# Four places for the high parts of weight slots, splits one slot further ahead, and an earlier expert output split

## What is computed

```python
def swiglu(t, w_gate, w_up, w_down):
    return (jax.nn.silu(t @ w_gate) * (t @ w_up)) @ w_down

def even_layer(...):
    u = rmsnorm(h, norm_mix);  proj = u @ w_in            # 9 slots of weights
    ...                                                   # mixing
    h = h + jnp.concatenate([y_a, y_b], axis=-1) @ w_out  # 4 slots
    return h + swiglu(rmsnorm(h, norm_ffn), ffn_wg, ffn_wu, ffn_wd)   # 33 slots

def odd_layer(...):
    u = rmsnorm(h, norm_mix);  proj = u @ w_in            # 12 slots
    ...
    h = h + jnp.concatenate([y_c, y_d], axis=-1) @ w_out  # 4 slots
    t = rmsnorm(h, norm_ffn).reshape(b * s, d)
    return h + moe_swiglu(t, router, moe_wg, moe_wu, moe_wd).reshape(b, s, d)

def moe_swiglu(t, router, w_gate, w_up, w_down):
    ...
    for e in range(N_EXPERTS):
        out = out + combine[:, e:e + 1].astype(t.dtype) * swiglu(t, w_gate[e], w_up[e], w_down[e])
    return out
```

## Time and profile before

| what | value |
|---|---|
| median of three runs | 2070.26 us |
| the profiled execution, its own time | 2068.16 us |
| its span in the trace | 2066.4 us |
| PE busy | 1895.6 us (92%) |
| DVE busy | 1449.9 us (70%) |
| ACT busy | 1134.7 us (55%) |
| chain that ended last | PE 82%, DVE 8%, ACT 4%, issue 3%, DMA 2% |
| read from memory | 464.58 MB, 225 GB/s over the span |
| mean granted TensorE clock | 0.959 of full speed |

### The profile page before, as it was taken

One profiled execution on the slowest core, in us unless ns is written; L12 is line 12 of the kernel. 1 busy time (PEld: TensorE's weight loads), 2 busy tenths in 40 slices (PEclk: granted clock), 3 DMA queues, 4 the chain that ended last, 5 costly groups with the idle time before them and its releaser, 6 DMA issues.

```text
span 2066.4 us, 27904 instructions
## 1 busy us (share of the span) xinstructions
PE 1895.6 (92%) x11188; PEld 1651.4 (80%) x11190; DVE 1449.9 (70%) x1458; ACT 1134.7 (55%) x1180; POOL 36.5 (2%) x84
## 2 busy tenths in 40 slices
PE   5969979999978699999999999999999997898997
PEld 4948869998867578788887888888888885888887
DVE  3777543445455478888888888888888886495484
ACT  4531223333344366776767676776766675554552
POOL 0010000000002000000000000000000000010010
PEclk9999989999999799999999999999999998899999
DMA  7200033454320378988889898888988895333331
GB/s 286 103 0 1 1 123 143 184 184 163 123 102 1 143 303 342 360 347 347 353 338 361 342 360 345 338 361 329 373 339 352 353 359 235 106 121 142 123 123 41
DMA packets 63775, 467.43 MB, mean 226 GB/s; under 512 B 7200, under 2 KB 7328, under 8 KB 7328
## 3 DMA queue, kind: packets, MB, share of 16 engines
q1 hardware_dynamic: 63648, 465.66, 57.9%
HBM read 464.58 MB, written 1.05 MB: 225 GB/s over the span
## 4 chain that ended last, share of the span: by engine, by line
PE 82%; DVE 8%; ACT 4%; issue 3%; DMA 2%; POOL 0%; SPq 0%; DVEq 0%; ACTq 0%
PE bank L511 80%; PE bank L521 2%; DMA weight_ring<-w_dram 2%; DVE split_ring L1693 1%; DVE squares L1679 1%; ACT split_ring L1214 1%; ACT moe_pair_high L1214 1%; ACT arena L1214 1%; DVE ycat L1677 1%; ACT L1214 1%; DVE expert_out_low L2190 0%; DVE moe_pair_low L2165 0%; DVE arena L1731 0%; DVE arena L1732 0%; ACT squares L1214 0%
## 5 line engine op out<-in xcount | busy, mean ns | idle before, releaser
L2165 DVE TENSOR_TENSOR moe_pair_low<-weight_ring,moe_pair_high 128x2048 fp32r<-128x2048 f32 x225 | 507.2, 2285 | 22.3 <-ACT moe_pair_high L1214 21.7
L1214 ACT ACTIVATE moe_pair_high<-weight_ring 128x2048 fp32r<-128x2048 f32 x225 | 426.6, 1916 | 37.5 <-DMA weight_ring<-w_dram 35.9
L511 PE MATMUL bank<-operand_high,split_ring 128*128 128x256 f32 x2000 | 399.9, 290 | 27.4 <-DVE operand_low L1700 22.1
L1214 ACT ACTIVATE arena<-bank 128x256 f32<-128x256 f32 (+5 forms) x250 | 114.3, 464 | 471.8 <-PE bank L511 442.6
L511 PE MATMUL bank<-moe_pair_high,operand_high 128*128 128x512 f32 x896 | 353.9, 395 | 9.1 <-DVE operand_low L2172 7.5
L511 PEld LDWEIGHTS bank<-operand_high,split_ring 128*128 128x128 f32 x2000 | 330.9, 197 | 31.7 <-issue 25.3
L511 PE MATMUL bank<-moe_pair_high,operand_low 128*128 128x512 f32 x896 | 352.6, 394 | 0.0
L511 PE MATMUL bank<-moe_pair_low,operand_high 128*128 128x512 f32 x896 | 350.1, 391 | 0.0
L1693 DVE TENSOR_TENSOR split_ring<-weight_ring,split_ring 128x2048 fp32r<-128x2048 f32 x78 | 178.4, 2290 | 211.5 <-ACT split_ring L1214 211.3
L511 PE MATMUL bank<-operand_low,split_ring 128*128 128x256 f32 x896 | 258.4, 288 | 0.0
L1214 ACT ACTIVATE split_ring<-weight_ring 128x2048 fp32r<-128x2048 f32 x78 | 148.9, 1912 | 159.2 <-PE bank L511 158.3
(11 more groups left out here) (283 smaller groups left out, 2661.8 us busy)
## 6 DMA issues: line engine op xcount, KB each, us to landing
weight_ring<-w_dram SPq DMA_DIRECT2D x381, 1024.0 KB, 6.9
arena<-w_dram SPq DMA_DIRECT2D x55, 1024.0 KB, 4.8
constants<-const_dram SPq DMA_DIRECT2D x1, 3124.0 KB, 17.8
parameters<-param_dram SPq DMA_DIRECT2D x1, 2896.5 KB, 24.2
hT<-x_dram SPq DMA_DIRECT2D x1, 1024.0 KB, 4.8
out_dram<-squares SPq DMA_DIRECT2D x1, 1024.0 KB, 3.9
constants<-const_dram SPq DMA_DIRECT2D x1, 128.0 KB, 4.6
parameters<-param_dram SPq DMA_DIRECT2D x1, 54.5 KB, 4.5
```

What stands on the lines that cost most here:

```text
L511: return pe.matmul(out, lhsT, rhs, start=start, stop=stop, skip_group_check=True)
L1214: return act.activation(out, in_, f, **kw)
L2165: tt(low_, raw_, high_.bitcast(F32), ALU.subtract).then_inc(moe_split, 1)
```

## The change

The high parts of all slots from 9 on get four places: the two of `late_high` and the two of `whi`. Slot n's high part so waits for slot n - 4 instead of n - 2. In the first output projection, the FFN and the second input projection, ACT and DVE take each slot's split one slot earlier. The extra split at the end of the first output projection is DVE's part of slot 15, behind `h_ready`; that at the FFN's end is slot 48's, behind slot 47's. In the second output projection one split fewer is left. In the experts' loop DVE's low parts of the output move ahead of the gate slot's low part. Loads, PE's program and the arithmetic are as before.

```diff
-            if not late and N_IN0 <= n < N_IN0 + 2:
-                return late_high[n - N_IN0]
+            if not late and n >= N_IN0:
+                return (late_high[0], late_high[1], whi[1], whi[0])[(n - N_IN0) % 4]
             return high_of[late][n % len(high_of[late])]
...
-                before = n - len(high_of[late])
+                before = n - (2 if n < N_IN0 and not late else 4)
                 if before >= 0 and (late or not N_IN0 <= n < N_IN0 + N_OUT):
                     act.wait_ge(*consumed[late, before])
...
-            for n in range(N_IN0 + 3, N_IN0 + N_OUT + 2):
+            for n in range(N_IN0 + 3, N_IN0 + N_OUT + 3):
                 hi(n)
             norm(1, 1)
             operand_hi(uT_, 1)
 
             w0 = N_IN0 + N_OUT
             for i in range(1, FFN_STEPS):
+                hi(w0 + 3 * i)
                 act.wait_ge(S["ffn_gu"], i)
-                hi(w0 + 3 * i - 1)
                 h = (i - 1) % 2
                 a_(sigb[h], banks[h][:, :], ACT.Silu).then_inc(S["ffn_sig"], 1)
-                hi(w0 + 3 * i)
                 hi(w0 + 3 * i + 1)
+                hi(w0 + 3 * i + 2)
             act.wait_ge(S["ffn_gu"], FFN_STEPS)
             a_(sigb[0], banks[0][:, :], ACT.Silu).then_inc(S["ffn_sig"], 1)
             w1 = w0 + N_FFN
-            hi(w1 - 1)
             hi(w1)
             hi(w1 + 1)
+            hi(w1 + 2)
...
-                    hi(w1 + 2 + 2 * i + n)
+                    hi(w1 + 3 + 2 * i + n)
...
             operand_hi(yc_)
-            hi(N_EARLY - 2)
             hi(N_EARLY - 1)
...
             st.say(dve.memset(tiny[:, 135:136], 0.0), "h_ready")
+            lo(N_IN0 + N_OUT + 2)
...
             for i in range(1, FFN_STEPS):
-                lo(w0 + 3 * i - 1)
+                lo(w0 + 3 * i)
                 ffn_step((i - 1) % 2, i)
-                lo(w0 + 3 * i)
                 lo(w0 + 3 * i + 1)
+                lo(w0 + 3 * i + 2)
             ffn_step(0, FFN_STEPS)
             w1 = w0 + N_FFN
-            lo(w1 - 1)
             lo(w1)
             dve.wait_ge(S["ffn_down"], FFN_STEPS + 1)
...
             lo(w1 + 1)
+            lo(w1 + 2)
...
-            for n in range(w1 + 2, w1 + N_IN1 + 2):
+            for n in range(w1 + 3, w1 + N_IN1 + 3):
                 lo(n)
...
-            residual(w1 + N_IN1 + 2)
+            residual(w1 + N_IN1 + 3)
...
                         moe_lo("down", q - 1)
-                    if q + 2 < QN:
-                        moe_lo("gate", q + 2)
                     if e and j == 1:
                         expert_out(e - 1)
                     if q + 2 < QN:
+                        moe_lo("gate", q + 2)
                         moe_lo("up", q + 2)
```

## The result

The changed kernel took 2048.44 us (median of 4 runs, 2047.08 to 2049.83) against 2068.84 us for the kernel before (4 runs, the three from above and one of 2067.41, 2062.81 to 2072.01): ratio 0.9905, 95% interval 0.988 to 0.9929. The prediction was 2050.5 us, in a range of 2043 to 2060. The profiled execution of after took 2047.08 us with a span of 2045.3, so 21.1 us less than the profiled one of before.

What follows compares the result with a forecast made beforehand. PE was taken as the bound, busy 1895.6 of 2066.4 us, so only its 171 idle us could be won. 4.8 + 6.1 − 2.3 + 0 + 9.0 = 17.6 us off 2068.16 gave 2050.5 us, range 2043 to 2060.

Steps and rivals of the forecast that it cites:

- (a): End of first output projection: slot 14 split earlier, less PE idle before the norm; gain 4.8 us, between 4.2 and 6.5.
- the commoner: Norm sums behind 2.09 us of idle: 5.38 us seen twice, 3.69 once; 5.4 taken, gaining 0.6 us instead of 2.3.
- (b): Entry of the FFN: slot 15's wait of 4.33 us and 1.8 us of low clock go; gain 6.1 us.
- (c): End of the FFN: one more split on DVE delays the norm's reciprocal; loss 2.3 us, bounds 0 and 4.
- (d): Second layer's input and output projections: PE doesn't wait for a split there; zero, ±0.5 us.
- (e): Experts' loop: output's low parts ahead of the gate's remove a PE stall, 1.29 us seven times; gain 9.0 us.
- The experts' stall: Rival: the stall returns at the up slot's low part or late loads; 2059.5 us, half 2055; lost or halved 0.10.
- The seams: Rival: late landings, not splits, bind the dense seams; 2055.3 us, or 2061.4 with slot 16 late; chance 0.06.
- The slower rival: Experts: output's low parts wait for ACT and delay the up slot; 2078.5 us at 2.7 us excess; chance 0.02.
- 7x: Cost in the slower rival: each expert pays an excess x, giving 2059.5 us + 7x.

Runs made afterwards that it cites:

- after_again: The changed kernel as it is, measured once more on another chip: 2048.33 us, ratio 0.992 to the kernel before.
- seam_a_only: The kernel before, with only slots 13 and 14 given late_high and waiting for the slot four before them: 2057.46 us, ratio 0.9965.
- dense_only: The changed kernel with the experts' loop in the order of the kernel before: 2055.52 us, ratio 0.9954.
- experts_last: The changed kernel with the expert output's low parts moved behind both weight slots' low parts: 2084.02 us, ratio 1.0099.
- run 8: The changed kernel, with low parts of slots 47 and 48 ahead of DVE's wait for the last FFN product: 2040.92 us, ratio 0.9885.
- run 4: The kernel before, waits and orders kept, with high parts from slot 13 on in late_high's two places: 2061.61 us, ratio 0.9984.
- run 7: The same run as experts_last: the changed kernel, expert output's low parts behind both weight slots' low parts, 2084.02 us.
- runs 5 to 8: Kernel before with FFN high parts in arena, 2065.26 us; changed kernel with slots 13, 14 held back, 2052.28 us; experts_last, 2084.02 us; run 8, 2040.92 us.

## Why the prediction was right, and where its terms were off

The forecast's mechanisms all came about, at their places, and its range held the time. By its own steps:

*(a), predicted 4.8, measured 6.5.* The idle part is exact, 6.29 to 2.09 us, with slot 15's split under its cover at no cost. The step that was mis-sized is "I take 5.4, the commoner": the sums took 3.69 us, from 5.98, so 2.3 us and not 0.6. The text called the choice between the two values luck. How far that holds, the 14 profiled executions show: each has an output projection of this kind at four places, and PE idles 2.1 us behind it in all of them (at the first place only where the change's waits are in). At this seam all seven executions with that gap (after, after_again, seam_a_only, dense_only, experts_last and both of the version of run 8) show 3.69. At the second all 14 show 5.38. At the third three show 3.69 and eleven 5.38. At the last, seven show 3.69 (as before in rows 6) and seven 5.38, as here in seam_a_only:

```profile
2039.05 5.38 PE L513 MATMUL bank<-squares,constants 128*128 128x256 f32 x16 [2.08 <-ACT squares L1216]
```

The Trainium skill, "TensorE: Matmul & The Clock Gate", Part 1, says that how many matmuls of the same kernel run cold varies with the phase of a free-running window. The third and the last place agree with it, as far as the same sums behind the same gap come out both ways; the first two don't vary. So neither the gap nor the place alone sets the value, and "the commoner" was a guess that missed by 1.7 us; the step's upper end, 6.5, is what came. What sets the value wasn't tried.

*(b), predicted 6.1, measured 7.4.* 4.33 us of idle and 1.8 of low clock are gone as said. The remaining 1.2 us are no wait at all but the shorter slots of run 4. "In the middle of a dense stage nothing is to be won" was right for waits and wrong for time: it took a slot's 5.76 us as fixed.

*(c), predicted a loss of 2.3, measured 2.1 and 0.8.* PE's gap grew from 5.64 to 7.75 us, and the wf matmuls behind it from 5.29 to 6.12. The reciprocal came 9.4 us after slot 47's low part began, 9.5 were named. What the step didn't ask is whether the split had to stand there: run 8 puts it into idle time ahead, and gets all of it back and more.

*(d), predicted 0 ± 0.5, measured −0.9*, and −1.7 without the 0.8 of wf. It was not taken apart, and it isn't clear of the scatter: from the wf matmuls to the second norm sums after took 158.3 us and dense_only, the same program in this stage, 160.6. Half of the slots lying in `late_high` would fit a gain.

*(e), predicted 9.0, measured 9.9 for the seven steps.* They went from 9.83 us (9.90 the first) to 8.43, 1.40 and not 1.29. The base was mis-read: the neighbour taken for the comparison, 8.54 us, is an even step, and the stalled one is odd; the odd steps beside it take 8.43. A further 1.0 us is four other steps of before, 0.1 to 0.45 us longer than their like in after, with late weights (`moe_pair_low`, two waits). They are no gain of the change: in the six other executions with the old order of the experts these steps are as short as in after. The last 0.8 us are small: 0.3 in the first step, 0.2 in the router, the rest hundredths.

*The rivals.* The experts' stall didn't come back elsewhere: the up slot's low part kept its slack, since the weight slots kept their start, and the loads kept pace at 349 GB/s. The seams were bound by the splits: ACT did stand 2.80 us for slot 14's landing, but with the copy at 282.15 the split could end at 286.4, 5.3 us before the last product does. The slower rival had no source; run 7 shows what it would have cost, dearer per microsecond than the 7x that was reckoned, because a stall of 3.35 us also takes the clock.

*The sum* was 17.6 us against 21.1 in the profiled executions and 20.4 in the medians. The difference of 3.5 is 1.7 of (a), 1.3 of (b), 0.2 of (c), 0.9 of (d) and 2.7 of (e) (1.0 of it before's own late weights), less 3.25 at the start and the end of the program, which no edit touches. The forecast that got a chance of 0.80 is called a gain of 14 to 23 us in one place, while the range itself stands for 8 to 25; the measured gain lies in both.

## What to carry to other kernels

Price a move by both what it frees and what it now stands in front of, and then look for idle time of the same engine just ahead of it: here the one split that cost 3 us stood behind a 6.7 us hole in its own queue. Read a stalled step against its like (same parity, same place in the loop), not against its neighbour. And an idle gap of PE is paid twice where it takes the clock, which behind 2.1 us came out either way: price it from rows with gaps of that length, and where they show two values, carry both.

## What the runs showed of the hardware that was not expected

Where the high parts lie in SBUF changes the pace of PE with no wait anywhere: a slot takes 5.76 us with them in `split_ring` or in the arena, 5.65 in `late_high`, 5.68 in `late_high` moved by 11 or 256 columns (one execution of each). No cause is shown. What a gap of PE does to the clock isn't set by its length alone: behind 2.1 us of idle the same sums took 3.69 us at one seam and 5.38 at another in every execution, and at the program's last seam 3.69 in seven executions and 5.38 in seven. In the experts the clock fell to 0.61 behind 3.35 us and stayed at 1.00 behind 1.15. And the scatter of this kernel's runs goes with its clock: the 17 runs of before beside runs 5 to 8 go from 2056.53 us at a mean granted clock of 0.968 to 2070.38 at 0.957, and of all runs of before beside an experiment the ten with a mean clock of 0.963 lie between 2062.2 and 2065.3 us.
